# Second layer of a two-layer trunk: gates between the projection's tiles, norm and gate inside the scans, output projection without transposes

## The reference, cut to what matters

```python
h = _rms(x, norm_w[1, 0]) * (1.0 + sc1) + sh1
u = h @ w_in                                   # 3360 columns
gq, gk, gv, gg, gaf, gab, hq, hff, hfb, hi, hg = _split(u, ...)
la_f = log_sigmoid(gaf @ gla_wa2[0] + gla_ba2[0]) / 16     # GLA: log decay, forward; la_b alike
f_f = lb + (1.0 - lb) * sigmoid(hff)                       # HGRN: decay log(f_f), key 1 - f_f; f_b alike
o_c = _bidir(q, k, k, v, v, la_f, la_b, ...)               # 4 heads, gated recurrence both ways, chunks
o_d = _bidir(qh, 1 - f_f, 1 - f_b, ih, ih, log f_f, log f_b, ...)   # 4 heads
y_c = _rms(o_c, gla_norm_w) * silu(gg)                     # norm over the 128 values of a head
y_d = _rms(o_d, hgrn_norm_w) * silu(hg)
x = x + g1 * (concat(y_c, y_d) @ w_out)
```

## Time and profile before

| what | us |
|---|---|
| median of 3 runs | 4070.31 |
| the runs | 4053.73 to 4113.91 |
| the profiled execution | 4050.31 |
| its span | 4048.6 |
| `n1a`, from its first DMA issue | 72.62 |
| `in1` | 361.22 |
| `gates` | 77.10 |
| `lin` | 437.44 |
| `fin` | 55.14 |
| `out` | 122.02 |

### The profile page before, as it was taken

One profiled execution on the slowest core, in us unless ns is written; L12 is line 12 of the kernel. 1 busy time (PEld: TensorE's weight loads), 2 busy tenths in 40 slices (PEclk: granted clock), 3 DMA queues, 4 the chain that ended last, 5 costly groups with the idle time before them and its releaser, 6 DMA issues. The chain is left out here.

```text
span 4048.6 us, 57029 instructions
## 1 busy us (share of the span) xinstructions
PE 3462.1 (86%) x22074; PEld 3125.9 (77%) x22074; DVE 1911.0 (47%) x3698; ACT 1087.7 (27%) x2053; POOL 292.0 (7%) x300
## 2 busy tenths in 40 slices
PE   5997673889699999999589975999756899999997
PEld 2997352669499999999389964777655899989996
DVE  4001565652555655565610015656554555565554
ACT  3111224660422112211321224434322212211220
POOL 1001351000100000000101110111111000000000
PEclk7998786999799999999799986989678999999998
DMA  6212303000311001100332215211020101110101
GB/s 261 92 75 73 117 1 119 2 22 21 121 52 42 33 32 53 43 32 27 139 135 80 79 66 231 86 62 62 22 68 16 59 32 49 41 38 32 53 32 52
DMA packets 77806, 268.49 MB, mean 66 GB/s; under 512 B 10736, under 2 KB 23920, under 8 KB 68960
## 3 DMA queue, kind: packets, MB, share of 16 engines
q1 hardware_dynamic: 68816, 236.27, 16.4%
q0 software_dynamic: 8720, 28.54, 1.9%
HBM read 217.23 MB, written 47.54 MB: 65 GB/s over the span
## 5 line engine op out<-in xcount | busy, mean ns | idle before, releaser
L83 PE MATMUL ffn__bank<-hf__h_lo,ffn__up_hi 128*128 128x384 f32 x2112 | 710.6, 336 | 64.1 <-DVE ffn__up_lo L515 59.2
L84 PE MATMUL ffn__bank<-hf__h_hi,ffn__up_lo 128*128 128x384 f32 x2112 | 709.3, 336 | 0.0
L85 PE MATMUL ffn__bank<-hf__h_hi,ffn__up_hi 128*128 128x384 f32 x2112 | 709.1, 336 | 0.0
L83 PEld LDWEIGHTS ffn__bank<-hf__h_lo,ffn__up_hi 128*128 128x128 f32 x2112 | 399.5, 189 | 67.0 <-DVE ffn__up_lo L515 48.9
L83 PE MATMUL ffn__bank<-ffn__g_lo,ffn__dn_hi 128*128 128x384 f32 x1056 | 381.4, 361 | 57.1 <-DVE all__x_t L564 34.6
L84 PEld LDWEIGHTS ffn__bank<-hf__h_hi,ffn__up_lo 128*128 128x128 f32 x2112 | 399.5, 189 | 0.0
L85 PEld LDWEIGHTS ffn__bank<-hf__h_hi,ffn__up_hi 128*128 128x128 f32 x2112 | 399.2, 189 | 0.0
L564 DVE SCALAR_TENSOR_TENSOR all__x_t<-ffn__bank,all__mods,all__x_t 128x128 f32<-128x128 f32 x704 | 345.0, 513 | 101.1 <-PE ffn__bank L85 98.9
L515 DVE TENSOR_TENSOR ffn__up_lo<-hf__raw,ffn__up_hi 128x1024 fp32r<-128x1024 f32 x88 | 107.7, 1225 | 600.8 <-ACT ffn__up_hi L399 600.8
L417 ACT ACTIVATE ffn__u<-ffn__bank 128x128 f32<-128x128 f32 (+1 forms) x352 | 133.2, 410 | 900.6 <-PE ffn__bank L85 882.2
L85 PE MATMUL ffn__bank<-ffn__g_hi,ffn__dn_hi 128*128 128x384 f32 x1056 | 357.2, 338 | 0.0
(11 more groups left out here) (321 smaller groups left out, 5969.0 us busy)
## 6 DMA issues: line engine op xcount, KB each, us to landing
hf__raw<-w_up SPq DMA_DIRECT2D x88, 512.0 KB, 3.8
ffn__dn_raw<-w_down SPq DMA_DIRECT2D x44, 512.0 KB, 4.1
n0a__ada_w<-w_ada SPq DMA_DIRECT2D x16, 1024.0 KB, 10.1
n1a__ada_w<-w_ada SPq DMA_DIRECT2D x16, 1024.0 KB, 7.9
u_t<-in__out_t POOLq DMA_DIRECT2D x24, 576.0 KB, 3.1
u_tok<-in__out_tok POOLq DMA_DIRECT2D x108, 128.0 KB, 2.2
hm__raw<-w_t SPq DMA_DIRECT2D x26, 512.0 KB, 3.8
in__wk_raw<-w_tok SPq DMA_DIRECT2D x12, 1024.0 KB, 5.6
```

Of the source, the lines that this page charges most:

```text
L83: pe.matmul(out, w_hi, v_lo, start=first, stop=False)
L84: pe.matmul(out, w_lo, v_hi, start=False, stop=False)
L85: return pe.matmul(out, w_hi, v_hi, start=False, stop=last)
```

## The change

- `n1a` also writes `x_t` to DRAM (`x_mid`), as SP's first DMA, 4608 KB. `x_t` is then free as working room until `out`.
- `in1` becomes `lin_project`: 19 feature tiles in the order 4 HGRN gates, rank columns, 2 q, 2 k, 2 HGRN q, 8 output gates (evicted with Silu), and 4 chunks. From tile 4 on, one of 21 gate pieces follows each bank: 12 pieces turn 384 tokens of f by three transposes and take Ln; 9 multiply 128 tokens of the rank columns by a 64x512 matrix (with the bias as a row), token-major at once, and take Abs, Exp, Ln. The block `gates` is gone.
- In `lin` the two operands of `outputs` are exchanged, so that results are feature-major, in `x_t`. Each of 24 blocks of 128 features by 384 tokens is finished in the scans: ACT squares it, PE sums with ones (`totals`, after j = 4), ACT takes Ln and Exp (`root`, between take and diagonals), DVE multiplies twice (`finish`), POOL loads the gate block. One block per unit in units 5 to 22, two each in 23 and in two rounds behind it. The sum's bank is one turn of the two that the exponents use. The block `fin` is gone.
- `out` becomes `out_project_t`: no transposes; its first two weight tiles are loaded in `lin`; its first tile runs over k outermost, behind the splitting of `y`; `x_t` is loaded back from `x_mid`.

```diff
+                if x_to:
+                    sp.dma_start(x_to, x_t[:, :, :]).then_inc(x_kept, 16)
...
@@ -1564,128 +1564,184 @@
 NL = len(LEVELS)
 
 
-def lin_gates(nc, tag, d, ident):
...
+LIN_TILES = ([("f", j) for j in range(4)] + [("a", 0)] + [("q", j) for j in range(2)] + [("k", j) for j in range(2)]
+             + [("hq", j) for j in range(2)] + [("gate", j) for j in range(8)])
+LIN_GATES = [("turn", j, b) for j in range(4) for b in range(NB)] + [("rank", c, 0) for c in range(NT)]
+GATES_FROM = 4
+GW = 4 * P
...
+def lin_project(nc, tag, d, stored, h_hi, h_lo, room, ident, raw, arrived):
...
+    kept_from = 5
+    x, k_out, a_t = room[:, 0:4, :], room[:, 4, :], room[:, 5, :]
+    log1 = room[:, 6, 0:2 * GW].rearrange("p (s n) -> p s n", s=2)
+    g = room[:, 7, 0:2 * GW].rearrange("p (s n) -> p s n", s=2)
...
+                def evict(t, b):
+                    kind, j = LIN_TILES[t]
+                    c = slice(b * BLK, (b + 1) * BLK)
+                    act.wait_ge(t_mm, NB * t + b + 1)
+                    src = ps[3 * (t % 2) + b][:, 0:BLK]
+                    if kind == "f":
+                        op = act.activation(x[:, j, c], src, ACT.Sigmoid)
+                    elif kind == "a":
+                        op = act.activation(a_t[:, c], src, ACT.Copy)
+                    else:
...
+                        if kind == "gate":
+                            op = act.activation(out_t[:, t % 2, c], src, ACT.Silu)
...
+                def logs(m):
+
+                    kind, j, b = LIN_GATES[m]
+                    src = ps[6 + m % 2]
+                    act.wait_ge(gate_mm, m + 1)
+                    if m >= 2:
+                        act.wait_ge(g_lo_done, m - 1)
+                    if kind == "turn":
+                        act.activation(g[:, m % 2, 0:BLK], src[:, 0:BLK], ACT.Ln).then_inc(gate_read, 1)
+                        return
+                    act.activation(log1[:, m % 2, :], src[:, :], ACT.Abs).then_inc(gate_read, 1)
+                    act.wait_ge(gate_read, m + 1)
+                    act.activation(log1[:, m % 2, :], log1[:, m % 2, :], ACT.Exp, scale=-1.0).then_inc(exp_done, 1)
+                    act.wait_ge(exp_done, m - n_turn + 1)
+                    act.activation(log1[:, m % 2, :], log1[:, m % 2, :], ACT.Ln, bias=1.0).then_inc(log_done, 1)
...
+                        evict(t, b)
+                        m = gate_at(t, b)
+                        if m is not None:
+                            if m >= 1:
+                                high(m - 1)
+                            logs(m)
+                            if m == n_gates - 1:
+                                high(m)
...
+                def forget(j):
+                    dve.wait_ge(t_out, NB * (j + 1))
                     dve.tensor_scalar(x[:, j, :], x[:, j, :], lb[:, j, 4:5], lb[:, j, 3:4], ALU.mult, ALU.add)\
                         .then_inc(f_done, 1)
                     dve.wait_ge(f_done, j + 1)
-                    dve.tensor_scalar(k[:, j, :], x[:, j, :], -1.0, 1.0, ALU.mult, ALU.add).then_inc(k_done, 1)
...
+                    if j >= 1:
+                        dve.wait_ge(k_kept, 16 * j)
+                    dve.tensor_scalar(k_out, x[:, j, :], -1.0, 1.0, ALU.mult, ALU.add).then_inc(k_done, 1)
+                    dve.wait_ge(k_done, j + 1)
+                    dve.tensor_scalar(x[:, j, :], x[:, j, :], 2.0 ** -63, None, ALU.max).then_inc(floored, 1)
...
+                def gate(m):
+                    kind, j, b = LIN_GATES[m]
+                    bank = ps[6 + m % 2]
+                    if m >= 2:
+                        pe.wait_ge(gate_read, m - 1)
+                    if m - 2 >= n_turn:
+                        pe.wait_ge(neg_done, m - 1 - n_turn)
+                    if kind == "turn":
+                        pe.wait_ge(floored, j + 1)
+                        for c in range(BLK // P):
+                            at = b * BLK + c * P
+                            last = pe.transpose(bank[:, c * P:(c + 1) * P], x[:, j, at:at + P], ident[:, :])
+                    else:
+                        pe.wait_ge(a_ready, 1)
+                        last = pe.matmul(bank[:, :], a_t[0:P // 2, j * P:(j + 1) * P], wa[:, :], start=True, stop=True)
+                    last.then_inc(gate_mm, 1)
...
+                        last.then_inc(t_mm, 1)
+                        if gate_at(t, b) is not None:
+                            gate(gate_at(t, b))
...
+def lin_finishes():
+
+    out = [[] for _ in range(LIN_PAIRS * 6 + 2)]
+    for k in range(6 * LIN_PAIRS):
+        pair, r = divmod(k, 6)
+        out[6 * pair + 5 + r if pair + 1 < LIN_PAIRS else 6 * pair + 5 + r // 2].append(k)
+    return out
+
+
+def lin_bank_turns(n_units, finishes):
+
+    order = [("e", n, i) for n in range(2) for i in range(PIECES_LIN)]
+    for n, items in enumerate(finishes):
+        ahead = n + 2 < n_units
+        order += [("e", n + 2, i) for i in range(CH) if ahead]
+        order += [("f", k, 0) for k in items]
+        order += [("e", n + 2, i) for i in range(CH, PIECES_LIN) if ahead]
+    return {use: x for x, use in enumerate(order)}
...
+    def block_of(k):
+
+        pair, r = divmod(k, 6)
+        b = NB - 1 - r // 2
+        return pair, r // 2, r % 2, 2 * pair + r % 2, slice(b * UW, (b + 1) * UW)
...
+                def load_gate(k):
+                    _, _, _, head, cols = block_of(k)
+                    if k >= 3:
+                        pool.wait_ge(finished, k - 2)
+                    pool.dma_start(gate[:, k % 3, :], d["u1_t"][4 + head, :, cols]).then_inc(gate_in[k % 3], 16)
...
+                def square(k):
+                    pair, m, h, head, cols = block_of(k)
+                    act.wait_ge(y_done[BWD], 2 * (pair * per_item + m) + h + 1)
+                    if k >= 2:
+                        act.wait_ge(summed, turn_of["f", k - 2, 0] + 1)
+                    act.activation(sq[:, k % 2, :], y[:, head, cols], ACT.Square).then_inc(squared, 1)
+
+                def root(k):
+                    x = turn_of["f", k, 0]
+                    act.wait_ge(summed, x + 1)
+                    if k >= 2:
+                        act.wait_ge(weighed, k - 1)
+                    act.activation(inv[:, k % 2, :], ps[x % 2][:, 0:UW], ACT.Ln, bias=eps[:, 0:1], scale=1.0 / LIN_V)\
+                        .then_inc(fact, 1)
+                    act.wait_ge(fact, x + 1)
+                    act.activation(inv[:, k % 2, :], inv[:, k % 2, :], ACT.Exp, scale=-0.5).then_inc(rooted, 1)
...
+                for n in range(n_units + 2):
+                    for z in finishes[n]:
+                        square(z)
...
+                    if 1 <= n <= n_units:
                         take(n - 1)
+                    for z in finishes[n]:
+                        root(z)
...
-                        pe.matmul(ps[3][:, c * P:(c + 1) * P], att[:, n % 2, h, c, :],
-                                  v[:, it % 2, c0 + c, h * LIN_V:(h + 1) * LIN_V], start=(c == 0), stop=False,
-                                  skip_group_check=True)
+                        pe.matmul(ps[3][:, c * P:(c + 1) * P], v[:, it % 2, c0 + c, h * LIN_V:(h + 1) * LIN_V],
+                                  att[:, n % 2, h, c, :], start=(c == 0), stop=False, skip_group_check=True)
                     for c in range(CH):
...
+                def totals(k):
+
+                    x = turn_of["f", k, 0]
+                    pe.wait_ge(squared, k + 1)
+                    pe.wait_ge(fact, x - 1)
+                    pe.matmul(ps[x % 2][:, 0:UW], ones[:, :], sq[:, k % 2, :], start=True, stop=True)\
+                        .then_inc(summed, 1)
...
+                        if j == 4:
+                            for z in finishes[n]:
+                                totals(z)
...
+                def finish(k):
+                    _, _, _, head, cols = block_of(k)
+                    ys = y[:, head, cols]
+                    dve.wait_ge(rooted, k + 1)
+                    dve.scalar_tensor_tensor(ys, ys, norm_w[:, head:head + 1], inv[:, k % 2, :], ALU.mult, ALU.mult)\
+                        .then_inc(weighed, 1)
+                    dve.wait_ge(weighed, k + 1)
+                    dve.wait_ge(gate_in[k % 3], 16 * (k // 3 + 1))
+                    dve.tensor_tensor(ys, ys, gate[:, k % 3, :], ALU.mult).then_inc(finished, 1)
...
+def out_project_t(nc, tag, l, d, x_t, w_raw, w_arrived, mods):
...
+                for k in range(KT):
+                    sp.wait_ge(y_lo_done, k + 1)
+                    sp.dma_start(x_t[:, k, :], d["x_mid"][:, k, :]).then_inc(x_in[k], 16)
+                    if k == 1:
+                        load_w(2)
+                        load_w(3)
...
+                    act.activation(y_hi[:, k, :], x_t[:, k, :], ACT.Copy).then_inc(y_hi_done, 1)
+                    if k == 0:
+                        split(1)
+                for n in range(2, KT):
...
+                    if n == 0:
+                        for k in range(KT):
```

(19 more changed lines are left out.)

538 lines of the change are left out of this document (309 added, 229 removed).

## The result

| | median us | runs | ratio to before |
|---|---|---|---|
| before | 4062.02 | 4046.18 to 4113.91 | 1 |
| changed | 4126.59 | 4119.09 to 4162.05 | 1.017 (1.013 to 1.022) |

The change makes the kernel 1.7% slower. 3985 us was forecast with a range up to 4055: wrong, and on the wrong side. The rival "the clock falls in the scans", which had 0.05 and 4155 us, is what happened, though the first fall stands behind another wait than the one it named. The profiled execution has a span of 4132.4 us and a mean clock of 0.888; before it was 4048.6 us and 0.915.

What follows compares the result with a forecast made beforehand. PE was taken to bound in1 (busy 347 of 361 us) and most of lin (401 of 437). The terms summed to -75.4 us from the profiled 4050.3, 3975; 10 added for a typical run gave 3985 us, range 3925 to 4055.

Steps and rivals of the forecast that it cites:

- the clock falls in the scans: Rival for lin: PE idling 3.6 us in forward units brings half clock; all 18 units give 4155 us; chance 0.05.
- n1a: Block n1a: small tensors wait behind the residual's store, so the whole block moves, +9.6 us (bounds 0 and 12.3).
- in1: Block in1: four chunks replaced by eight feature tiles, turned pieces and rank products on PE, +10.0 us.
- gates: Block gates is gone from the path, -77.1 us.
- fin: Block fin is gone from the path, -55.1 us.
- out: Block out: first product after 3.8 us instead of 18.6, since the weights are there, -14.8 us.
- lin: Block lin: forward roots and sums 38.6, the other nine units 1, the tail 12.5 us; together +52 us.
- The forward waits: lin, nine forward units: PE waits 3.5 to 4.3 us for ACT's root; with the sums 38.6 us.
- Finishing costs DVE 1.1 us a unit beside PE: lin: finishing hidden beside PE, nothing added; 20 us over 18 units if DVE's idle time were gone.
- the row of `ssd`: Evidence against the clock falling: in ssd PE is busy 12.04 of 15 us at 1.00, as idle as these units.

Runs made afterwards that it cites:

- best: split_front plus the residual's store as SP's last DMA of n1a and ACT's wait for it in in1: 4018.0 us, 0.987 of before.
- store_tail: Changed kernel with the residual's store as SP's last DMA of n1a instead of its first, one run: 4174.7 us.
- split_defer: split with the residual's store as SP's last DMA of n1a and its wait in in1: 3926.1 us, 0.963 of before.
- root_only: Changed kernel finishing no block, but ACT makes Ln and Exp with table loads on a constant in units 5 to 23: 4049.0 us, 0.994 of before.
- split_early: split with DVE's finishing of a block back at the end of the unit: 3980.9 us, 0.979 of before.
- split: Changed kernel, sum behind third exponent piece, Ln before first take, Exp before second, finishing in middle of next unit: 3930.4 us, 0.969 of before.
- before_root: Kernel before plus ACT's Ln and Exp with table loads on a constant between take and diagonals, units 5 to 23: 4197.2 us, 1.031 of before.
- no_norm: Changed kernel without the norm and gate of all 24 blocks; exchanged operands stay: 3944.7 us, 0.964 of before.
- sums_only: Changed kernel without roots, finishing and gate loads; squares and sums stand: 3929.8 us, 0.969 of before.
- late: Changed kernel with DVE's finishing moved from the unit's end to the middle of the next unit: 4095.0 us, 1.006 of before.
- both: Changed kernel with Exp in place of the root's Ln (no table loads) and finishing in the next unit's middle: 4052.2 us, 0.983 of before.
- split_front: split with ACT's Exp of the fourth exponent piece ahead of the six diagonals instead of behind them: 4026.2 us, 0.989 of before.

## Why the prediction was wrong

*`n1a`.* Right in size (+11.7; bounds 0 and 12.3) and in cause. ACT's Silu came 14.4 us after the first issue (12.7 forecast), and the small tensors landed with the store ahead of them. The timeline of ACT, then two DMA issues (KB, us to landing):

```profile
1976.76 0.41 ACT L132 ACTIVATE n1a__ada_c_act<-n1a__ada_c 128x256 f32<-128x256 f32 x1 [46.57 <-DMA n1a__ada_norm_w<-norm_w]
...
x_mid<-all__x_t SPq DMA_DIRECT2D x1, 4608.0 KB, 13.4
n1a__ada_c<-c_t SPq DMA_DIRECT2D x1, 8.0 KB, 13.0
```

The Silu is 11.3 us later in its block than before (14.4 against 3.1), and the block 11.7 us longer; the store had landed 71 us before the block ended. The expectation of best, that the store costs 9.6 us at either end because the block waits for it, holds only for the store at the end (store_tail, 82.2 us). With the store behind the weights and its wait in `in1`, the block takes 74.5 us (split_defer).

*`in1`.* Right (370.8, forecast 371.2), and PE never waited in the rank tiles. Inside, the sizes cancel: nine rank products from 2159.1 to 2202.7 us come every 5.44 us, so each adds 1.28 us to the 4.16, not 0.87; a bank with three transposes takes 4.51, so they add 0.35, not 0.5. By these the sum for the block is +11.9 and not +10.0, of which 2.3 us did not show. ACT takes 5.8 us a rank piece (5.6 forecast).

*`gates`, `fin`, `out`.* Right, the first two by construction. The first product of `out`, which answers to the earlier trace rows, comes 3.7 us into the block where 3.8 were forecast:

```profile
3065.40 0.66 PE L83 MATMUL out__bank<-out__y_lo,out__w_hi 128*128 128x384 f32 x1 [12.90 <-DVE out__y_lo L2479]
```

*`lin`.* Three steps, of which the last decided.

1. The forward waits were sized well: 3.5 to 4.3 us forecast, 4.43 in root_only at full clock. Two table loads cost 1.28 us each and nothing behind them, as the earlier trace rows said; the drain of 1.38 us that the Trainium skill adds to a switch ("ScalarE: Activation LUTs", What ACT_TABLE_LOAD costs) is in no row here.
2. "Finishing costs DVE 1.1 us a unit beside PE", costed at nothing since DVE has idle time, failed. The idle time lies ahead of the picks of the later levels, not at the seam between two units, where the change put the work; there PE waits 1.43 us. The forecast had named 20 us for this case; split_early against split shows 40 to 50, the falls of the clock included.
3. "The clock falls in the scans (0.05)" is the step that failed. Against it stood the row of `ssd`, 12.04 of 15 us busy at 1.00. That row says how much PE idled, not in what pieces: PE's longest waits in it are 1.10 us, and windows of the same length in the same block are not at full clock, one of them with PE busy throughout.

```profile
485.00:500.00 15.00, 15.00 (x67) 0.60 0.00 0
...
560.00:575.00 15.00, 13.34 (x73) 0.89 0.01 1
...
590.00:605.00 15.00, 5.50 (x24) 0.59 0.00 0
```

One favourable window had been taken for the rule, and so the sum held nothing for the clock. The runs show in its place: clock back at 1.00 without the waits (split), gone with them alone (before_root). The Trainium skill ("TensorE: Matmul & The Clock Gate", HAM oscillation) says that PE's idle gaps bring half clock back, and by it the rival deserved much more than 0.05; the runs agree, though most of the waits here are shorter than the gaps that the section warns of. That the rival's 4155 us lies near 4126.59 is in part luck: it counted 18 units at 9 to 10 us each (its own counts, 123 and 73 instructions in 12 us, give 11); measured, a whole unit at half clock costs 12.5 us (28.8 less 16.3), eleven of the 18 are wholly at half clock and six in part. It also had the first fall behind ACT's root, where it came behind DVE's finishing.

What it cost: against split's `lin` (433.8 us, PE busy 391.5) the changed one (644.2, busy 581.7) is 210 us longer. PE's idle time in it is 20 us more (62.5 against 42.3); the other 190 us are the same 3576 products at the lower clock.

**Open.** Stretches of half clock also come where the longest wait in the units ahead is 0.67 us (and in best in unit 0, behind one of 0.63): before in unit 8, no_norm in 14, sums_only and late in 3, both, root_only and store_tail in 2. The windows of PE in units 7 and 8 before:

```profile
2611.33:2626.96 15.63, 14.96 (x150) 1.00 0.47 162
2626.96:2653.94 26.98, 26.98 (x150) 0.50 0.13 44
```

The seven falls come 0.1 to 1.0 us after the start of a unit, and each time the unit ahead was one with the wait of 0.67 us, never one whose longest wait is 0.55. So 0.67 us may not be harmless; that was not tried. Such a stretch lasts from 14 us (sums_only) to 150 (store_tail), and a profile that has one is longer by that chance. Waits of 1.10 us in `ssd` had a fall behind one of the five between 545 and 590 us only. What decides whether a wait is followed by a fall, and when the clock comes back, from within one unit in split_early to five units in the changed kernel, was not tried.

## What to carry to other kernels

Where PE is kept just busy by other engines, price a new wait by the clock first and by its own length second: here waits once in a unit of 16 us cost several times themselves. Nine waits, 3.7 us longer each (33 us), cost 94 us in before_root, and 20 us of idle time came with 190 us of slower products in the changed kernel. Before putting work on an engine "with idle time", read in the timeline where that idle time stands, and put the work into it, in pieces if need be; the split root, table loads and all, made no wait of PE longer. A large store belongs behind the small loads that an engine waits for, and its wait where its buffer is first overwritten, not at the end of the block that issues it.

## What the runs showed of the hardware

- Seen behind PE's longest wait in a unit: 4.3 to 4.4 us, the clock falls in each first forward unit (before_root, late); 1.7 us, the same (both); 1.43 us, in six of eight units (split_early); 1.04 us, 14 of 22 units below full clock for a part (split_front). With 0.67 us in forward units and 0.55 and 0.35 us in others, in no unit before the last two in split and split_defer, but once in each of seven other profiles, always in the unit behind a wait of 0.67 us.
- At half clock the waits for DVE vanish (1.43 us in unit 6 of the changed kernel, none in units 7 to 12) and those for ACT shrink (4.4 to 2.8 us in root_only), so a trace at half clock hides what made the clock fall: the cause is at the edge where it falls, not in the stretch behind it.
- Three of the 24 DVE operations of L2372 started with one of POOL (1.00 us) and took 1.40 us, the other 21 took 0.56; five of L2314 took 1.16 to 1.31 us beside one of POOL, where the others take 0.35. Not every kind is slowed: the pick of L2334 beside POOL took 0.59 us, as without it.
